# Second mixer's turned banks, work at the stage borders and the last norm put in another order: a float32 network of two blocks on one Trainium2 core

## Chip, core and metric

The kernel runs on one core of a Trainium2 chip. The metric is the device time of one execution in microseconds (us). Everything is float32. The weights come from HBM in each execution; activations stay in SBUF.

## What is computed

The input is 256 tokens of width 1024. A first block (a SwiGLU "ffn1", a mixer of RWKV-7 and dilated attention, a SwiGLU "ffn2") is followed by two layers of a second block, which the change is about. Cut to its core:

```python
def second_layer(x, i):                                   # i = 0, 1
    z = h @ w_in                                          # dq, dk, dv, cq, ckv, kr, gates
    o_a = rmsnorm((softmax(dq1 @ dk1.T) - lam * softmax(dq2 @ dk2.T)) @ dv)   # 8 heads
    o_b = softmax(q_mla @ k_mla.T) @ v_mla                # 8 heads, from low-rank cq, ckv
    m = g_a * (o_a @ w_branch_diff) + g_b * (o_b @ w_branch_mla)
    x = layernorm(ALPHA * x + m @ w_out)                  # "norm 2i"
    f = swiglu(x) if i == 0 else moe(x)                   # dense 2816, or 8 experts of 3584, top 2
    e = sigmoid(x @ w_ple_gate) * (p[i] @ w_ple_proj)     # p[i]: 256 x 256 embedding
    x = layernorm(ALPHA * x + f + e)                      # "norm 2i + 1"
```

## The kernel before

The 256 tokens are two tiles `t` of 128. `h_cm` holds the activations with channels on partitions (8 groups `k`), `x_tm` and `xn` with tokens on partitions. Every float32 product is two records per 128-row step in the trace, so a gate product of one token tile and 512 columns (8 groups) counts as 16 pieces. The program gives each engine its own list of instructions, in an order written out by hand, tied by semaphores; nothing reorders it at run time.

**Banks.** `next_bank()` deals the eight PSUM banks in turn. `fill` makes TensorE wait until the bank's last user has been copied out, `full` makes a reader wait for the product, `free` and `drained` tell and await the copy. ScalarE and VectorE share the copies.

**Weights.** One list, `stream`, names every slab of weights in the order of use; SyncE (SP) loads them into four slots in turn (line 2861), each load waiting for the last reader of the load four places ahead. Dense FFNs (`sp_ffn`) and the experts (`sp_experts`) load two pieces per unit of 256 hidden columns, of 2 MB and 1 MB.

**ffn2** (`dve_ffn`, `dve_unit`, line 608). 11 units; TensorE does the up products of unit u + 1, then the down product of unit u (`pe_up`, `pe_down`). VectorE multiplies gate and up when a unit's up products are ready, and then does `beside(u)`: an eleventh of the relative bias table (`dve_bias`, lines 1820 to 1828). After the last unit it adds the four result banks to `x_tm` (line 686); TensorE turns `x_tm` for the second block (line 394).

**Second mixer** (`pe_mixer2`, `act_mixer2`, `dve_mixer2`). For each pair of heads `a`: `dqk(a)` (query and key product), `diff_scores(a)` (line 1922), softmax on VectorE and ScalarE, and later `diff_out(a)`, which turns the weights into two banks (line 1931), waits until both are copied to `PT2` (ScalarE line 2090, VectorE line 2227) and multiplies them with the values (lines 1940, 1941). `mla_out(g)` does the same with three banks (lines 1966, 1976, 1978; copies in lines 2097 and 2252). Products of other weights (`dv`, `uq`, `ukv`, the gates `g2`) stand between. ScalarE takes its copies in its own fixed order: in `mla_out(1)` it copies the turned banks and the output, then takes the root of the mean squares (line 2147); VectorE inverts it (line 2276) and scales OA (line 2279), which `bdiff` reads. `pe_out` multiplies the merged branches with `w_out` (line 1637), and the embedding `ple` is turned (line 2047).

**Behind the mixer** (`pe_extras`, `dve_extras`). VectorE adds `w_out`'s products, takes the norm tile by tile (lines 2288, 1838 to 1844), TensorE turns `x_tm` (line 394), ScalarE and VectorE copy it to `h_cm`. Four gate products (`pg`) and four small projections (`pp`, all after them) follow, both through line 321; VectorE multiplies and adds them (lines 2350, 2352). In layer 0 the dense FFN follows in the seven-product form of line 443: it needs sums of the inputs and of each unit's weights, which VectorE makes (`dve_x_sums`, `dve_weight_sums`, lines 561 to 577) before TensorE's third product. In layer 1 a router goes between, and then 16 gather products and a transpose (line 2529, 2534), before which TensorE waits for all eight banks.

**Experts and tail.** 112 units (lines 2483, 2495), one pass. Last, the sums of expert 7 are turned (line 2509), copied by ScalarE (half 0) and VectorE (half 1) (line 2594), scattered by four products (line 2573) and, per token tile, added (line 2670), reduced to mean and variance (2671 to 2674), and normed in three operations of 1024 columns (2677, 2679, 2680). One DMA stores both tiles (line 2863).

## Time and profile before

| what | value |
|---|---|
| three runs | 2799.74, 2808.26 (median), 2810.09 us |
| the profiled execution | 2807.01 us; its span in the trace 2805.1 us |
| busy, share of the span | TensorE matmul 2696.7 us (96%), weight load 2272.9 (81%), VectorE 892.8 (32%), ScalarE 366.6 (13%), GpSimd 19.6 (1%) |
| mean granted TensorE clock | 0.993 |
| DMA | 601.6 MB, 214 GB/s over the span; in the slices of the experts 369 to 401 GB/s |

The span begins with the first instruction and ends with the last DMA. A row of a timeline or group gives the line of the kernel, engine, operation, out<-in by the program's names, sizes and a count of records; behind it, in brackets, the idle time of the engine before it and what ended that. PEclk is the share of the full TensorE clock that was granted. `SPq` is SyncE's DMA issue. The border between ffn2 and the second block lies at 943 us, layer 0 of the second mixer runs to 1239, layer 1 from 1499 to 1788, the experts from 1855 to 2782.

### The profile page before, as it was taken

Reading aid. Unit: us, or ns where it says so; the run is one execution under the profiler, and the core shown is the slowest. Engines: PE = TensorE matmul, PEld = TensorE weight load, DVE = VectorE, ACT = ScalarE, POOL = GpSimd, SP = SyncE. Lnnn points to the kernel's source line nnn. Section 1 sums busy time; section 2 is a strip of 40 time slices with the busy share of each in tenths; the row PEclk is TensorE's granted clock in tenths of the full one; section 3 lists DMA queues with packets and bytes.
Section 4 is the critical chain, followed back from the end, with each engine's and each line's share of the span. In section 5 each row is a group of like instructions: output and inputs, shape, how many; then the busy total and the mean of one; then the engine's idle time right before and its main releaser. Section 6 shows DMA issues by size and latency. Waiting matters only on the chain.

```text
span 2805.1 us, 73047 instructions
## 1 busy us (share of the span) xinstructions
PE 2696.7 (96%) x33424; PEld 2272.9 (81%) x33424; DVE 892.8 (32%) x1661; ACT 366.6 (13%) x827; POOL 19.6 (1%) x36
## 2 busy tenths in 40 slices
PE   7999999899999999999999999999999999999997
PEld 6877778877677768857876788479999999999997
DVE  5341554623776433425443334320000000000003
ACT  1002232210100034200002241110000000000000
POOL 0000000000000000000000000000000000000000
PEclk9999999999999999999999999999999999999999
DMA  5434332022443424333445243259999999999995
GB/s 196 180 150 181 118 121 84 4 80 109 148 177 138 176 100 152 120 135 121 179 159 197 98 154 121 90 225 397 369 379 396 387 396 374 370 401 376 397 386 237
DMA packets 55573, 601.57 MB, mean 214 GB/s; under 512 B 6320, under 2 KB 6448, under 8 KB 9856
## 3 DMA queue, kind: packets, MB, share of 16 engines
q1 hardware_dynamic: 52128, 587.74, 53.5%
q0 software_dynamic: 3296, 11.57, 1.2%
q8 instruction: 127, 2.08, 0.3%
q14 instruction: 22, 0.18, 0.0%
HBM read 595.48 MB, written 3.81 MB: 214 GB/s over the span
## 4 chain that ended last, share of the span: by engine, by line
PE 91%; DMA 4%; DVE 3%; issue 1%; ACT 1%; SPq 0%; DVEq 0%; ACTq 0%
PE bank L311 21%; PE bank L2483 19%; PE bank L443 10%; PE bank L2495 9%; PE bank L475 7%; PE bank L321 6%; PE bank L464 5%; DMA slot<-in_experts 4%; PE bank L1637 3%; PE bank L1203 2%; PE bank L1623 1%; PE bank L2529 1%; PE bank L931 1%; PE bank L1224 1%; PE bank L1296 0%
## 5 line engine op out<-in xcount | busy, mean ns | idle before, releaser
L2483 PE MATMUL bank<-arena,slot 128*64 128x96 f32 x14336 | 615.4, 246 | 10.1 <-issue 6.1
L2483 PEld LDWEIGHTS bank<-arena,slot 128*64 128x64 f32 x14336 | 601.4, 137 | 14.0 <-issue 13.9
L311 PE MATMUL bank<-h_cm,slot 128*128 128x256 f32 (+2 forms) x2032 | 447.5, 381 | 0.3 <-ACT h_cm L350 0.3
L311 PEld LDWEIGHTS bank<-h_cm,slot 128*128 128x128 f32 (+2 forms) x2032 | 383.9, 190 | 63.2 <-issue 8.2
L2495 PE MATMUL bank<-ff,slot 128*64 128x96 f32 x7168 | 320.8, 246 | 14.6 <-DMA slot<-in_experts 8.2
L2495 PEld LDWEIGHTS bank<-ff,slot 128*64 128x64 f32 x7168 | 306.5, 137 | 17.6 <-issue 17.6
L2643 DVE TENSOR_TENSOR ff<-ff,bank 128x192 f32<-128x192 f32 x112 | 39.6, 354 | 797.4 <-PE bank L2483 797.4
L475 PE MATMUL bank<-slot,ff 128*128 128x512 f32 x528 | 231.5, 592 | 0.0
L475 PEld LDWEIGHTS bank<-slot,ff 128*128 128x128 f32 x528 | 98.8, 190 | 112.4 <-issue 111.9
L464 PE MATMUL bank<-h_cm,slot 128*128 128x256 f32 x704 | 153.7, 379 | 0.4 <-ACT h_cm L352 0.4
L464 PEld LDWEIGHTS bank<-h_cm,slot 128*128 128x128 f32 x704 | 133.7, 190 | 22.5 <-issue 4.9
L1828 DVE SCALAR_TENSOR_TENSOR arena<-arena 128x384 f32<-128x384 f32 x264 | 142.7, 613 | 1.2
L321 PE MATMUL bank<-slot,h_cm 128*128 128x512 f32 (+1 forms) x320 | 136.4, 585 | 1.3 <-ACT h_cm L350 1.1
L2607 ACT ACTIVATE ff<-bank 128x192 f32<-128x192 f32 x112 | 37.1, 331 | 768.5 <-PE bank L2483 768.5
L311 PE MATMUL bank<-arena,slot 128*128 128x256 f32 x608 | 133.2, 380 | 0.0
L443 PE MATMUL bank<-arena 128*128 128x128 f32 x1056 | 126.9, 277 | 4.2 <-DVE arena L574 4.2
L311 PEld LDWEIGHTS bank<-arena,slot 128*128 128x128 f32 x608 | 115.0, 190 | 18.3 <-issue 2.9
L443 PEld LDWEIGHTS bank<-arena 128*128 128x128 f32 x1056 | 123.1, 194 | 4.5 <-DVE arena L574 4.5
L321 PEld LDWEIGHTS bank<-slot,h_cm 128*128 128x128 f32 x320 | 61.2, 194 | 71.2 <-issue 70.4
L443 PEld LDWEIGHTS bank<-h_cm,slot 128*128 128x128 f32 x704 | 81.8, 192 | 10.7 <-issue 10.7
L443 PE MATMUL bank<-h_cm,slot 128*128 128x128 f32 x704 | 82.2, 275 | 1.2 <-DVE h_cm L365 1.2
L1637 PE MATMUL bank<-slot,arena 128*128 128x512 f32 x192 | 82.9, 592 | 0.0
(402 smaller groups left out, 2025.4 us busy)
## 6 DMA issues: line engine op xcount, KB each, us to landing
slot<-in_experts SPq DMA_DIRECT2D x112, 2048.0 KB, 9.0
slot<-in_experts SPq DMA_DIRECT2D x112, 1024.0 KB, 9.2
slot<-in_ffn SPq DMA_DIRECT2D x22, 2048.0 KB, 9.2
slot<-in_ffn SPq DMA_DIRECT2D x22, 1024.0 KB, 4.9
slot<-in_dense SPq DMA_DIRECT2D x11, 2048.0 KB, 8.9
slot<-in_dqk SPq DMA_DIRECT2D x8, 2048.0 KB, 8.1
slot<-in_g SPq DMA_DIRECT2D x8, 2048.0 KB, 7.8
slot<-in_w_in_rkv SPq DMA_DIRECT2D x6, 2048.0 KB, 7.9
```

The lines of the kernel that those rows point to most:

```text
L311: ins = pe.matmul(ps[0:m, j * S:(j + 1) * S], w[:, k * width + c0:k * width + c0 + m], rhs[:, k, :], start=k == 0, stop=k == ks - 1)
L321: ins = pe.matmul(ps[:, 0:n], lhs[:, k, t * P:(t + 1) * P], w[:, k * width + c0:k * width + c0 + n], start=start and k == 0, stop=stop and ...
L443: ins = pe.matmul(ps[:, g, :], left[q][:, k, g, :], right[q][:, k, :], start=k == 0, stop=k == 3)
L464: ins = pe.matmul(bank[:, m * S:(m + 1) * S], slot[s][:, c0:c0 + P], h_cm[:, k, :], start=k == 0, stop=k == KD - 1)
L475: ins = pe.matmul(PS[4 + 2 * t + half][:, :], hidden[par][:, kk, t * P:(t + 1) * P], slot[s][:, kk * D + half * 512:kk * D + half * 512 + ...
L1203: ins = pe.matmul(ps[rows, h * width + c0:h * width + c0 + 64], left(rows, a, p, i), right(rows, a, p, i), start=True, stop=True)
L1637: ins = pe.matmul(ps[:, :], src[:, k, t * P:(t + 1) * P], w[:, k * 512:(k + 1) * 512], start=k == 0, stop=k == KD - 1)
L1828: v.scalar_tensor_tensor(BIAS[:, h, :], REACHED[r], STEP_NOW[:, r * 8 + h:r * 8 + h + 1], BIAS[:, h, :], ALU.mult, ALU.add).then_inc(done, 1)
L2483: ins = pe.matmul(bank[64 * c:64 * c + 64, m * PLACES:(m + 1) * PLACES], slot[s][:, c0:c0 + 64], QUEUE[:, e, k, :], start=k == 0, stop=k = ...
L2495: ins = pe.matmul(PS[down_bank(e) + d // 4][64 * c:64 * c + 64, (d % 4) * PLACES:(d % 4 + 1) * PLACES], slot[s][:, c0:c0 + 64], ff[:, 2 + ...
L2607: act.activation(ff[:, par, 0:2 * PLACES], PS[par][:, 0:2 * PLACES], ACT.Silu).then_inc(silu_ready, 1)
L2643: v.tensor_tensor(ff[:, 2 + par, 0:2 * PLACES], ff[:, par, 0:2 * PLACES], PS[2 + par][:, 0:2 * PLACES], ALU.mult).then_inc(hidden_ready, 1)
```

## The change

Seven edits. (1) In the second mixer the turning transposes become functions of their own (`diff_turn`, `mla_turn`), and the next scores, or half of the last gate product, are put between them and the product that uses the turned banks. (2) In ffn2 `beside(u)` comes before unit u's multiply; `beside(1)` also before unit 1's. (3) The embedding is turned before `w_out`, copied by VectorE in the mixer, and half of the projections go before the norm's transposes, the other half between the gate products; their slab is loaded first. (4) In layer 0 VectorE makes the dense FFN's input sums and first weight sums before it multiplies the gate products. (5) The gathers start in the bank that is next in turn and wait for each bank by itself; two banks are passed over in layer 1. (6) The scatter is ordered by half, and the last norm has two operations of 1024 columns instead of three. (7) Each token tile is stored by itself; ScalarE releases the first store.

```diff
@@ -246,12 +246,12 @@
                             ("bdiff_", 0), ("bdiff_", 1), ("out2_", 0), ("out2_", 1)):
                 stream.append(((f"{name}{l}", n), dram[f"{name}{l}"][n], dram[f"{name}{l}"].shape[2]))
             if l == 0:
+                slabs("pleproj_0")
                 slabs("plegate_0")
-                slabs("pleproj_0")
                 stream.append(("ffn", "dense", U_DENSE))
             else:
+                slabs("pleproj_1")
                 slabs("plegate_1")
-                slabs("pleproj_1")
                 stream.append(("experts", "experts", N_EXPERTS * U_EXPERT))
...
@@ -618,28 +618,33 @@
         def dve_ffn(dve, name, beside=lambda u: None):
 
             n0 = unit_base[name]
-            for j in range(2):
-                dve_unit(dve, (n0 + j) % 2, n0 + j, True)
-                beside(j)
+            dve_unit(dve, n0 % 2, n0, True)
+            beside(0)
+            beside(1)
+            dve_unit(dve, (n0 + 1) % 2, n0 + 1, True)
             with dve.Fori(1, U_DENSE // 2) as i:
                 for j in range(2):
+                    beside(i * 2 + j)
                     dve_unit(dve, (n0 + j) % 2, i * 2 + n0 + j, False)
-                    beside(i * 2 + j)
+            beside(U_DENSE - 1)
             dve_unit(dve, (n0 + U_DENSE - 1) % 2, n0 + U_DENSE - 1, False)
-            beside(U_DENSE - 1)
...
+        def dve_unit_sums(dve, name, j, i=0):
+            at = first_load[name] + 2 * j
+            dve_weight_sums(dve, U_DENSE * IN_SEVEN[name] + j + 2 * i, at // SLOTS + 1 + i, at % SLOTS)
+
+        def dve_first_sums(dve, name, turned):
+            h_written(dve, turned)
+            dve_x_sums(dve, IN_SEVEN[name])
+            dve_unit_sums(dve, name, 0)
...
@@ -1923,13 +1932,15 @@
                                             KDF[64 * m:64 * m + 64, 2 * a + j, 0:n], start=True, stop=True)
                         filled(ins, key)
 
-            def diff_out(a):
+            def diff_turn(a):
                 pe.wait_ge(named("diff_weights"), 4 * l + a + 1)
                 for b, blocks in enumerate((range(0, 4), range(4, 6))):
                     ps = fill(pe, ("dt", l, a, b), next_bank())
                     for i, f in enumerate(blocks):
                         ins = pe.transpose(ps[:, i * P:(i + 1) * P], WD[:, f // 3, (f % 3) * P:(f % 3 + 1) * P], ident)
                     filled(ins, ("dt", l, a, b))
+
+            def diff_out(a):
                 for b in range(2):
                     drained(pe, ("dt", l, a, b))
                 for t in range(T):
...
@@ -1991,12 +2004,14 @@
                     ins = pe.matmul(ps[:, j * S:(j + 1) * S], ones, LSQ[:, k, :], start=k == ks[0], stop=k == ks[-1])
             filled(ins, ("ls", l))
             dqk(1)
+            diff_turn(0)
+            diff_scores(1)
             diff_out(0)
-            diff_scores(1)
             dv(1)
             dqk(2)
+            diff_turn(1)
+            diff_scores(2)
             diff_out(1)
-            diff_scores(2)
             pe.wait_ge(named("lat_ready"), l + 1)
             w = slab(pe, (f"uq_{l}", 0))
             for b in range(2):
...
                 product_tm(pe, ("uv", l, t), next_bank(), w, 1024, 512, 512, LAT[:, NQ:, :], NKV, t)
             released((f"ukv_{l}", 0), ("uv", l, 1))
             g2(0)
+            diff_turn(3)
+            mla_scores(0)
             diff_out(3)
-            mla_scores(0)
             g2(1)
+            mla_turn(0)
+            mla_scores(1)
             mla_out(0)
-            mla_scores(1)
             g2(2)
             pe.wait_ge(named("oa_squared"), l + 1)
             for b in range(4):
                 ps = fill(pe, ("dn", l, b), next_bank())
                 filled(pe.matmul(ps[:, :], ones, QD[:, 2 * b:2 * b + 2, :], start=True, stop=True), ("dn", l, b))
+            mla_turn(1)
+            g2_bank(3, 0)
             mla_out(1)
-            g2(3)
+            g2_bank(3, 1)
             for g in range(2):
                 drained(pe, ("mo", l, g))
             w = slab(pe, (f"bmla_{l}", 0))
@@ -2039,13 +2059,13 @@
                     product_cm(pe, ("bd", l, 4 * s + 2 * j), next_bank(), w, 512,
                                [(2 * j * P, P), ((2 * j + 1) * P, P)], OA, KD)
                 released((f"bdiff_{l}", s), ("bd", l, 4 * s + 2))
-            pe_out(pe, f"out2_{l}", KDF, "merged", 4 * l)
             pe.wait_ge(named("ple_loaded"), 16 * (l + 1))
             ps = fill(pe, ("pleT", l), next_bank())
             for k in range(2):
                 for t in range(T):
                     ins = pe.transpose(ps[:, k * S + t * P:k * S + (t + 1) * P], PLE_TM[:, t, k * P:(k + 1) * P], ident)
             filled(ins, ("pleT", l))
+            pe_out(pe, f"out2_{l}", KDF, "merged", 4 * l)
 
         def act_softmax(act, l, name, groups, base):
...
@@ -2280,6 +2300,8 @@
             for tile in range(0, 16, 2):
                 drained(dve, ("g2", l, tile))
             dve_merge(dve, ch, ("bm", l), ("bd", l), gates2, KDF, QD, (8, 0))
+            ps = full(dve, ("pleT", l))
+            free(v.tensor_copy(PLE_CM, ps[:, :].rearrange("p (k s) -> p k s", s=S)), ("pleT", l))
 
         def dve_add_mix(dve, l, t, half):
             key = (f"out2_{l}", half, t)
...
@@ -2310,22 +2336,24 @@
                     ins = pe.matmul(ps[:, c0:c0 + 8], const(lhs, P), RT[4][:, t, :], start=start, stop=stop_)
                 filled(ins, ("rank",))
 
+            drained(pe, ("pleT", l))
+            projection(0)
+            pe_layernorm(pe, 2 * l)
             for s in range(2):
+                if s:
+                    projection(1)
+                    released((f"pleproj_{l}", 0), ("pp", l, 1, 1))
                 w = slab(pe, (f"plegate_{l}", s))
                 for t in range(T):
                     product_tm(pe, ("pg", l, s, t), next_bank(), w, 512, 0, 512, h_cm, KD, t,
                                turned=("turn", 2 * l + 1) if s == t == 0 else None)
                     if l == 1 and s == t == 0:
                         router()
+                        for held in range(2):
+                            next_bank()
                 released((f"plegate_{l}", s), ("pg", l, s, 1))
                 if l == 1 and s == 0:
                     ranks()
-            drained(pe, ("pleT", l))
-            w = slab(pe, (f"pleproj_{l}", 0))
-            for s in range(2):
-                for t in range(T):
-                    product_tm(pe, ("pp", l, s, t), next_bank(), w, 1024, 512 * s, 512, PLE_CM, 2, t)
-            released((f"pleproj_{l}", 0), ("pp", l, 1, 1))
 
         def act_extras(act, ch, l):
             for s in range(2):
@@ -2338,9 +2366,9 @@
 
         def dve_extras(dve, ch, l):
             v = nc.vector
-            ps = full(dve, ("pleT", l))
-            free(v.tensor_copy(PLE_CM, ps[:, :].rearrange("p (k s) -> p k s", s=S)), ("pleT", l))
-            if l == 1:
+            if l == 0:
+                dve_first_sums(dve, "dense", ("turn", 1))
+            else:
                 dve_router(dve, ch)
             for s in range(2):
                 for t in range(T):
...
             L, n0 = first_load["experts"], unit_base["experts"]
             gathered, scattered = named("moe_bank_filled"), named("moe_scattered")
-            for b in range(8):
-                pe.wait_ge(psum_free[b], turns[b])
+            moe_from.append(rotation[0] + 1)
             assert 2 * U_EXPERT % SLOTS == 0
             with pe.Fori(0, passes(pe)) as p:
 
                 pe.wait_ge(named("ln_var"), p * T + T * LAST_NORM)
                 pe.wait_ge(named("pick_ready"), p + 1)
                 for j in range(GATHERS + TURNED):
-                    ps = PS[j % 8]
-                    if j >= 8:
+                    ps = PS[moe_first(j)]
+                    if j < 8:
+                        pe.wait_ge(psum_free[moe_first(j)], turns[moe_first(j)])
+                    else:
                         pe.wait_ge(named(f"moe_bank_read{j % 2}"), p * moe_reads(j % 2) + (j - 8) // 2 + 1)
                     if j < GATHERS:
                         k, h = divmod(j, 2)
@@ -2566,10 +2600,10 @@
 
                 pe_moe_turn(pe, p, N_EXPERTS - 1)
                 pe.wait_ge(hidden_ready, p * ALL_UNITS + n0 + ALL_UNITS)
-                for half in range(2):
-                    pe.wait_ge(sums_ready[half], p * N_EXPERTS + N_EXPERTS)
                 for b in range(4):
-                    t, half = divmod(b, 2)
+                    half, t = divmod(b, 2)
+                    if t == 0:
+                        pe.wait_ge(sums_ready[half], p * N_EXPERTS + N_EXPERTS)
                     pe.matmul(PS[b][:, :], RETURN[:, t * P:(t + 1) * P], SUMS[:, LAST, half * 512:half * 512 + 512],
                               start=True, stop=True).then_inc(scattered, 1)
...
@@ -2619,6 +2653,9 @@
                 for t in range(T):
                     act.wait_ge(named("ln_var"), p * T + T * LAST_NORM + t + 1)
                     act.activation(lstd[:, t:t + 1], lstd[:, t:t + 1], ACT.Sqrt).then_inc(named("ln_std"), 1)
+                act.wait_ge(named("out_row0"), p + 1)
+                act.copy(stat[:, 13:14], ident[:, 0:1])
+            act.copy(stat[:, 14:15], ident[:, 0:1]).then_inc(named("first_ready"), 1)
 
         def dve_experts(dve, ch):
...
+                tail = named("tail_step")
+
+                def tail_done(n):
+                    dve.wait_ge(tail, p * TAIL_STEPS + n)
+
+                def tail_add(t, half):
+                    c = slice(half * 512, half * 512 + 512)
+                    dve.wait_ge(named("moe_scattered"), p * 4 + 2 * half + t + 1)
+                    v.tensor_tensor(E_TM[:, t, c], E_TM[:, t, c], PS[2 * half + t][:, :], ALU.add).then_inc(tail, 1)
+
+                def tail_stats(t, half):
+                    v.bn_stats(bnst[:, t, 6 * half:6 * half + 6], E_TM[:, t, half * 512:half * 512 + 512]).then_inc(tail, 1)
+
+                def tail_var(t, n):
+                    v.tensor_copy(lstd[:, t:t + 1], bnst[:, t, 0:1])
+                    v.bn_aggr(bnag[:, t, :], bnst[:, t, :]).then_inc(tail, 1)
+                    tail_done(n)
+                    v.tensor_scalar(lstd[:, t:t + 1], bnag[:, t, 1:2], EPS, None, ALU.add).then_inc(named("ln_var"), 1)
+
+                def tail_rows(t, n):
+                    dve.wait_ge(named("ln_std"), p * T + T * LAST_NORM + t + 1)
+                    v.reciprocal(lstd[:, t:t + 1], lstd[:, t:t + 1]).then_inc(tail, 1)
+                    v.scalar_tensor_tensor(OUT[:, t, :], E_TM[:, t, :], bnag[:, t, 0:1], lnrow[:, 0, :], ALU.subtract, ALU.mult
+                                           ).then_inc(tail, 1)
+                    tail_done(n + 2)
+                    v.scalar_tensor_tensor(OUT[:, t, :], OUT[:, t, :], lstd[:, t:t + 1], lnrow[:, 1, :], ALU.mult, ALU.add
+                                           ).then_inc(named(f"out_row{t}"), 1)
+
+                for half in range(2):
+                    for t in range(T):
+                        tail_add(t, half)
+                tail_done(3)
+                tail_stats(0, 0)
+                tail_stats(0, 1)
+                tail_done(6)
+                tail_var(0, 7)
+                tail_stats(1, 0)
+                tail_stats(1, 1)
+                tail_done(9)
+                tail_var(1, 10)
+                dve.wait_ge(named("ln_rows"), 16 * 2 * (LAST_NORM + 1))
+                tail_rows(0, 10)
+                tail_rows(1, 12)
                 for t in range(T):
...
+                    dve.wait_ge(named(f"out_row{t}"), p + 1)
             dve.sem_inc(named("out_ready"), 1)
 
...
+            sp.wait_ge(named("first_ready"), 1)
+            sp.dma_start(out[:, 0, :], OUT[:, 0, :]).then_inc(named("out_stored"), 16)
             sp.wait_ge(named("out_ready"), 1)
-            sp.dma_start(out, OUT).then_inc(named("out_stored"), 16)
-            sp.wait_ge(named("out_stored"), 16)
+            sp.dma_start(out[:, 1, :], OUT[:, 1, :]).then_inc(named("out_stored"), 16)
+            sp.wait_ge(named("out_stored"), 32)
```

`mla_out` is divided as `diff_out` is, `dve_ffn_seven` no longer makes the first sums, `g2` is divided into `g2_bank(s, j)`, and the two halves of `projection(s)` are `product_tm` of the two token tiles.

## Rows read from the trace of the kernel before

**Rows 1.** Waits of TensorE, whole span: engine, line <- releaser: total us, times, longest us.
```profile
PE bank L2495 <- DMA slot<-in_experts: 8.2, 7, 2.1
...
PE bank L1940 <- ACT arena L2090: 5.0, 8, 0.8
...
PE bank L394 <- DVE x_tm L686: 3.4, 1, 3.4
...
PE bank L1976 <- DVE arena L2252: 3.3, 4, 0.8
```

**Rows 2.** Stretches: us, busy us of PE, PEld, DVE, ACT, POOL, clock, DMA share, GB/s.
```profile
1861.00:2777.00 916.00, 891.95 (x21306) 884.55 (x21304) 52.90 (x129) 44.21 (x125) 7.44 (x11) 1.00 0.96 385
...
1240.00:1241.00 1.00, 1.00 (x2) 0.34 (x1) 1.00 (x2) 0.98 (x2) 0.00 (x0) 0.50 0.88 377
```

**Rows 3.** Timeline of VectorE and TensorE, start of ffn2: start us, us, engine, line.
```profile
735.73 0.69 DVE L608 TENSOR_TENSOR ff<-ff,bank 128x512 f32<-128x512 f32 x1 [0.90 <-ACT ff L548]
...
750.80 0.69 DVE L608 TENSOR_TENSOR ff<-ff,bank 128x512 f32<-128x512 f32 x1
...
763.92 7.03 PE L475 MATMUL bank<-slot,ff 128*128 128x512 f32 x16
```

**Rows 4.** Chain of waits behind ffn2: start us, us, what.
```profile
946.67 3.75 PE bank L394 x16
...
950.42 35.78 PE bank L311 x160
```

**Rows 5.** Timeline of ScalarE and VectorE between MLA output and OA, layer 0.
```profile
1151.52 0.59 ACT L2099 COPY arena<-bank 128x512 f32<-128x512 f32 x1 [1.76 <-PE bank L1978]
...
1155.36 12.95 DVE L2276 RECIPROCAL arena<-arena 128x2048 f32<-128x2048 f32 x1 [5.90 <-ACT arena L2147]
...
1170.68 1.29 DVE L2279 TENSOR_SCALAR arena<-arena,cols 128x2048 f32<-128x2048 f32 x1
```

**Rows 6.** Timeline of TensorE, from embedding transposes to dense FFN, layer 0.
```profile
1234.24 0.60 PE L2047 MATMUL bank<-consts,arena 128*128 128x128 f32 x4
...
1237.63 1.09 PE L394 MATMUL bank<-consts,x_tm 128*128 128x128 f32 x8 [1.91 <-DVE x_tm L1844]
...
1239.27 29.19 PE L321 MATMUL bank<-slot,h_cm 128*128 128x512 f32 x64 [0.55 <-ACT h_cm L350]
...
1268.29 7.03 PE L321 MATMUL bank<-slot,arena 128*128 128x512 f32 x16
...
1281.95 5.47 PE L443 MATMUL bank<-arena 128*128 128x128 f32 x32 [3.06 <-DVE arena L574]
```

**Rows 7.** Timeline of VectorE, first input sum and last weight sum, dense FFN.
```profile
1276.88 0.69 DVE L561 TENSOR_TENSOR arena<-h_cm 128x512 f32<-128x512 f32 x1
...
1282.94 1.22 DVE L577 TENSOR_TENSOR arena<-slot,arena 128x1024 f32<-128x1024 f32 x1
```

**Rows 8.** Timeline of TensorE, gathers of the experts.
```profile
1831.94 22.60 PE L2529 MATMUL bank<-arena,x_tm 128*128 128x384 f32 x64 [2.50 <-issue]
```

**Rows 9.** Timeline of the tail; third, 1024-wide scalar_tensor_tensor of line 2439 (ns).
```profile
2784.13 0.69 DVE L2594 COPY arena<-bank 96x512 f32<-96x512 f32 x1 [1.09 <-PE bank L2509]
...
2786.10 0.69 DVE L2670 TENSOR_TENSOR arena<-arena,bank 128x512 f32<-128x512 f32 x1 [1.28 <-PE bank L2573]
...
L2439 DVE SCALAR_TENSOR_TENSOR arena<-arena x4: 1277/1281/1285, 2761.7 to 2765.5; 128x1024 f32<-128x1024 f32 x4
...
2797.21 0.81 DVE L2677 TENSOR_SCALAR arena<-arena,ff 128x1024 f32<-128x1024 f32 x1
...
2799.32 1.23 DVE L2680 TENSOR_TENSOR arena<-arena,xn 128x1024 f32<-128x1024 f32 x1
...
2800.79 0.35 SPq L2863 DMA_DIRECT2D out<-arena  x1
```

**Rows 10.** DMA issues of the page: size of one, median us to landing.
```profile
slot<-in_bdiff SPq DMA_DIRECT2D x4, 2048.0 KB, 7.8
...
slot<-in_pleproj SPq DMA_DIRECT2D x2, 1024.0 KB, 4.9
```

63 lines of the change are left out of this document (26 added, 37 removed).

## Prediction

> **What bounds the kernel now.** I read the waits of TensorE first, because its matmuls fill nearly the whole span: what it waits for is what can be won. The reader is to see that the waits are short and lie at borders: eight waits for a turned attention bank (5.0 us), four for the second kind (3.3), one for the bias work of VectorE (3.4) [rows 1]. Next come the stretches: the loop over experts takes 916 of 2805 us, and there TensorE (892) and the DMA engines (0.96) are both full; one microsecond of a border elsewhere shows TensorE at a granted clock of 0.50, the 1.2 GHz level, where nearly everything else has 1.00 [rows 2]. So the loop of experts is left as it is, and the change is worth what it takes from the borders, plus the slow clock behind them. The timelines of the borders give the terms. All sums are made against the profiled execution (2807.01 us, span 2805.1), which stands 1.25 us under the median of the three runs (2808.26).
>
> **Term A, the ffn2 stage.** Each `beside` is 750.80 - 735.73 - 0.6 = 14.5 us of VectorE [rows 3]. Two of them now precede unit 1's product: it ends at 736.4 + 2 x 14.5 + 0.7 = 766.0. TensorE wants it (`down` of unit 1) at 763.9, so a new wait of about 2.0 us appears; behind VectorE nothing else is queued, and ScalarE's next silu waits only for unit 0. A unit costs TensorE 20.7 us (up 64 x 0.215, down 16 x 0.43) and VectorE 15.2, so VectorE has caught up two units later, and the wait comes once. At the other end VectorE no longer has 14.5 us of bias after the last unit. `down` ends at 946.67 - 3.4 = 943.3 [rows 1, 4]; the first three additions then lie under `down` itself, the fourth takes 0.7 under the first eight transposes. A piece of 512 columns takes 0.43 us (16 in 7.03, with a drain of some 0.15 [rows 3]), one of 256 a half, one of 128 a quarter, 0.11. So sixteen transposes take 1.8 us against 3.4 + 3.75, and the product of 160 pieces 34.5 against 35.78. From 943.3 to the end of that product: 42.9 before, 36.4 after: 6.5 gained, 2.0 paid. **4.5**.
>
> **Term B, the two mixers.** In each layer, four `diff` and two `mla` turns now have scores (or, last, half a gate product) between the transposes and their use, at least 16 pieces of 0.1 us, while the copy of a bank takes 0.59 [rows 5]. The 5.0 and 3.3 us go [rows 1]. What is late next: the scores wait for ScalarE's copy of the `dqk` bank, done just as six transposes end; I take zero. Banks: laid out over the eight, each is reused at least one product after its copy. **8.3**, between 4 and 8.3. The last move delays something: the MLA output bank comes half a gate product (6.9 us) later, and ScalarE stands waiting for it, with the square root queued behind it, for which VectorE's reciprocal of 12.95 us waits. Before, the output bank ends at 1151.5 and OA is ready at 1172.0, 20.5 us later [rows 5]. After, TensorE goes on from the output with 6.9 (half gate) + 13.8 (`bmla`) = 20.7 us and then wants OA. A slack of 27.6 - 20.5 = 7.1 us shrinks to 0.2: cover still, but only just.
>
> **Term C, layer 0 behind the mixer.** Before [rows 6]: the products with `out2` end at 1234.4 (the embedding's transposes begin), gate product starts at 1239.27 (4.85 us later), 64 pieces in 29.0 instead of 27.5 (slow clock, 1.5), projections 6.9 to 1275.3; then 32 pieces of the FFN, a wait of 3.06 for the weight sums, and 32 pieces in 5.47, to 1287.25: 52.8 us. After: turning the embedding, now ahead of the products out, 0.45; half of the projections 3.43 and the first eight transposes 0.86 fill the norm's wait (z of the second tile is there after 3.2); second transposes to product 1.64 (1239.27 - 1237.63); gates 27.5; other projections 3.43; FFN's banks 0 to 3 free 1.4 later (0.6 of ScalarE, 0.7 of VectorE on the last piece; bank 2 is one of them); 64 pieces of 0.11, 7.15. Sum 45.9. **6.9**. The input and first weight sums move under the gate product: x sums and four weight sums run 1276.88 to 1284.16, 7.3 us [rows 7]. Before the first multiply they end at about the 19th microsecond, the second projection wants its bank at 20: no wait, under 1 us if the slab lands late. SP's queue: the projection's slab comes first, the second gate slab is asked for 6.9 us before the products out end and needed 20 us after; the first dense slab is behind it, asked for as before. POOL issues nothing new.
>
> **Term D, layer 1.** The same border gives 4.85 + 1.6 + 3.43 - 6.4 = 3.5. At the gathers, before: idle 2.5, then 64 pieces of 384 columns in 22.6, of which 20.6 at full clock [rows 8]. The wait for all banks (0.8) goes; I keep the 1.7 between bank and first gather, which nothing in the trace explains. 25.1 against 22.3: 2.8. **6.3**. The loads of experts start on the end of the first `up`, as before: the loop shifts as a whole.
>
> **Term E, the tail.** The first addition starts at 2786.10; the scatter now begins with ScalarE's half alone, which is turned four transposes (0.5) before the half that VectorE copies until 2784.8; so 0.5 sooner, bounds 0 and 0.7. From it to the last row was 14.45. After: additions paced by the scatter 3.3, four statistics 2.9, two variances 0.9, reciprocals 0.4, four `scalar_tensor_tensor` of 1024 at 1.28 with hops 5.2: 12.7. So 0.5 + 1.75. ScalarE's reply (0.2) is hidden under tile 1. Per tile 0.81 + 1.23 + 1.22 = 3.26 becomes 2.56 [rows 9]. The store ends 4.3 us after its issue; half the bytes save between 0 and 2.15: loads of 2 MB and 1 MB land in 7.8 and 4.9, so half a MB is worth 1.4, which I take [rows 10]. **3.7**. VectorE's two operations each read two tensors. The Trainium skill (VectorE: DVE Perf Modes, the perf-mode tier table) has fp32 `tensor_scalar` at two elements per cycle and `tensor_tensor` at one, so the change gives up the only fast pass; by its figures, halved for 1024, an estimate is 0.61 + 2 x 1.15 = 2.91 against 2.3, 0.6 saved per tile and not 0.7. The rows have the same two rates. For the store, the skill (DMA: Bandwidth & Descriptors, Anatomy of one DMA) states about 2.0 us fixed plus bytes at 436 GB/s; by that the half store would save 1.2.
>
> **Sum.** 4.5 + 8.3 + 6.9 + 6.3 + 3.7 = 29.7; 2807.0 - 29.7 = 2777.3, and as a median 1.25 more: 2778. The clock: I count no fall behind the waits that remain (2.0, 1.7, 1.4, 0.6), since the one of 2.1 us in the expert loop stood at 1.00 [rows 1, 2], while 3.4, 3.06, 2.5 and 1.91 with 0.55 were followed by a fall. Each fall costs 1.5 to 2.0.
>
> **Rivals.** (1) *The waits move.* The clock falls as often as before (four times 1.6), and half of B comes back as waits for `dqk` copies and banks. For it: the mixer's copies follow each other on one engine. Against: the eight-bank order. 29.7 - 6.4 - 4.2 = 19: 2789. (2) *OA comes late.* The slack of 0.2 is overdrawn by a table load of 1.28 and hops in both layers, and the FFN wait of 2.0 brings a fall: 3 + 1.6: 2782. (3) *Slower: the expert loop loses its balance with the DMA.* 112 units of 3.15 MB took 8.18 us each at 385 GB/s [rows 2]. Its loads begin in another slot order than before. If the DMA engines gave 366 GB/s, a unit would take 8.59, and 112 of them 46 us more: 2824. It decides from 0.27 us per unit, where all the gain is gone. Against: the order of loads after the first unit is unchanged, and TensorE itself needs 7.96 of the 8.18. (4) *It does not overlap.* The projection or the sums ahead are held by a bank or slab, so C and D give a third: 2787.
>
> **How the numbers follow.** Forecast 0.64, (1) 0.15, (2) 0.08, (4) 0.08, (3) 0.03, the last 0.02 among waits I do not see. A measurement of this kernel tells about 0.5% from no change, 14 us: 2794. Forecast, (2), nearly all of (4) and most of (1) lie under it: faster 0.91, same 0.06, slower 0.03. Range: up to rival (1) and the half of the runs' spread (10 us); down, 2778 - 5 for the spread and - 7 for the 1.7 at the gathers, the FFN bank wait, the store's bound and a better loop: 2766 to 2793.
>
> **What would show it.** Right: no waits of the lines that use turned banks; one new wait of about 2 us on the second `down` of ffn2; the gate products 6.4 us behind the products out with clock 1.00; no wait on the weight sums in the first dense unit; a first store under the work of tile 1. Wrong: a wait of `bdiff` on OA; clock 0.50 behind the borders; the loop from first expert product to last longer than 921 us.

## The result, and the profile after

The changed kernel takes 2775.97 us (median of 4 runs, 2770.60 to 2781.55) against 2807.60 in the runs beside it (2799.74 to 2810.09): a ratio of 0.9892, 95% interval 0.9864 to 0.992, so 1.1% faster, beyond the noise. Forecast were 2778 and 2766 to 2793. The profiled execution took 2774.82 us, span 2773.0, 32.1 under that of before.

TensorE's longest waits, and that of the second FFN, after the change (engine, line <- releaser: total us, times, longest):

```profile
PE bank L394 <- DVE xn L382: 16.6, 3, 12.9
PE bank L2511 <- issue: 8.3, 12, 1.3
PE bank L2523 <- DMA slot<-in_experts: 7.5, 6, 1.9
...
PE bank L475 <- DVE ff L608: 1.8, 1, 1.8
```

The waits for turned banks [rows 1] are gone, and that for the bias work at the FFN's end. One has come: `down` of unit 1, for VectorE's multiply. The timelines of the places where the prediction has a term, first the start and the end of ffn2 and of the first product behind it (start us, us, engine, line, shapes, xcount, idle before):

```profile
764.83 7.13 PE L475 MATMUL bank<-slot,ff 128*128 128x512 f32 x16 [1.76 <-DVE ff L608]
...
944.10 0.38 PE L394 MATMUL bank<-consts,x_tm 128*128 128x128 f32 x2
945.05 1.75 PE L394 MATMUL bank<-consts,x_tm 128*128 128x128 f32 x14 [0.57 <-DVE x_tm L691]
946.97 35.11 PE L311 MATMUL bank<-h_cm,slot 128*128 128x256 f32 x160 [0.17 <-ACT h_cm L354]
...
1139.49 1.47 PE L1977 MATMUL bank<-consts,arena 128*128 128x128 f32 x12
1140.81 7.07 PE L311 MATMUL bank<-h_cm,slot 128*128 128x256 f32 x32
1147.81 0.65 PE L1989 MATMUL bank<-arena 128*64 128x256 f32 x4
```

Against [rows 3, 4]: a wait of 1.76 where 2.0 was forecast; 3.75 us of slow transposes are 2.1 fast ones; but only two of them run before the wait of 0.57, not eight. The last three rows are the last turn of layer 0 (L1977), half a gate product, and the product over the turned banks, which starts without a wait. Next VectorE and ScalarE behind the MLA output of layer 0 [rows 5]:

```profile
1149.38 0.58 ACT L2119 COPY arena<-bank 128x512 f32<-128x512 f32 x1 [7.79 <-PE bank L1991]
...
1153.21 12.95 DVE L2296 RECIPROCAL arena<-arena 128x2048 f32<-128x2048 f32 x1 [11.92 <-ACT arena L2167]
...
1168.53 1.29 DVE L2299 TENSOR_SCALAR arena<-arena,cols 128x2048 f32<-128x2048 f32 x1
```

OA is ready at 1169.82. The product over it follows 20.73 us of other products (96 pieces) that follow one another from 1149.33, so it is wanted at 1170.06: 0.24 us of slack, where 0.2 was worked out. Then TensorE at the border of layer 0 [rows 6]:

```profile
1229.05 1.91 PE L394 MATMUL bank<-consts,x_tm 128*128 128x128 f32 x16
1231.51 13.97 PE L321 MATMUL bank<-slot,h_cm 128*128 128x512 f32 x32 [0.55 <-ACT h_cm L350]
1245.31 3.60 PE L321 MATMUL bank<-slot,arena 128*128 128x512 f32 x8
1248.75 13.90 PE L321 MATMUL bank<-slot,h_cm 128*128 128x512 f32 x32
1264.21 3.81 PE L443 MATMUL bank<-h_cm,slot 128*128 128x128 f32 x32 [1.57 <-issue]
```

The idle time of the norm is filled, the gate products run at full clock, and of the 3.06 us on the sums only 1.57 on bank 2 are left. Last the border of layer 1 and the gathers [rows 8], and three stretches of it (us, busy of PE, PEld, DVE, ACT, POOL, granted clock, DMA share, GB/s):

```profile
1769.49 7.10 PE L321 MATMUL bank<-slot,h_cm 128*128 128x512 f32 x16 [0.55 <-ACT h_cm L350]
1776.44 3.63 PE L2326 MATMUL bank<-arena,h_cm 128*128 128x8 f32 x32
1779.93 8.81 PE L321 MATMUL bank<-slot,h_cm 128*128 128x512 f32 x16
...
1806.86 20.80 PE L2563 MATMUL bank<-arena,x_tm 128*128 128x384 f32 x64
```

```profile
1774.00:1780.00 6.00, 6.00 (x40) 4.57 (x38) 0.98 (x1) 1.88 (x2) 1.06 (x2) 1.00 0.55 171
1780.00:1784.00 4.00, 4.00 (x7) 1.70 (x7) 3.00 (x18) 1.12 (x2) 0.00 (x0) 0.57 0.01 5
1784.00:1790.00 6.00, 6.00 (x23) 3.25 (x22) 1.12 (x8) 0.96 (x2) 0.00 (x0) 1.00 0.15 30
```

The gathers start without a wait and at full clock. But behind the router's 32 narrow matmuls (8 columns) the clock goes to the 1.2 GHz level, though TensorE was never idle: the same gate product takes 7.10 us ahead of them and 8.81 behind.

Where the 32.1 us went, each from the starts of products in both timelines: 1.0 ahead of everything that was changed; **A** 3.1; **B** 9.9; **C** 6.75; **D** 6.5; the expert loop, 926.97 before and 926.12 after, 0.85; **E** 4.4; less 0.4 in the first products of layer 1, which the clock fall around norm 1 meets at another point.

### The profile page after: what moved, and what is told of

Same layout as the page of the kernel before. It is cut to its first block, busy times and chain, and to the rows that moved or that the text cites. A ratio compares the mean times of both kernels' runs of the same rounds, so it can differ in the third digit from the quotient of the medians.

```text
span 2773.0 us, 73042 instructions
## 1 busy us (share of the span) xinstructions
PE 2689.7 (97%) x33424; PEld 2268.6 (82%) x33424; DVE 890.5 (32%) x1659; ACT 365.2 (13%) x829; POOL 19.6 (1%) x36
## 4 chain that ended last, share of the span: by engine, by line
PE 91%; DMA 4%; DVE 3%; issue 1%; ACT 1%; POOL 0%; SPq 0%; DVEq 0%; POOLq 0%; ACTq 0%
PE bank L311 21%; PE bank L2511 19%; PE bank L443 10%; PE bank L2523 9%; PE bank L475 8%; PE bank L321 6%; PE bank L464 4%; DMA slot<-in_experts 4%; PE bank L1642 3%; PE bank L1208 2%; PE bank L1628 1%; DVE arena L1833 1%; PE bank L2563 1%; PE bank L936 1%; PE bank L1229 1%
```

## The experiments

Stretches repeat from profile to profile to some 0.02 us where neither a wait nor the granted clock differs, while whole executions scatter by 10. So each experiment is read at its own stretch. These are TensorE's, in us, start to start: `down` of unit 0 to the transposes behind ffn2; those to the first product of layer 0; out product to the first dense `down`; the mixer of layer 0; gate product to the gathers; gathers to the first expert; and from the end of the last product to the end of the span.

```
kernel               ffn2  turn   border 0  mixer 0  gates 1  gathers  end
before             203.43  3.55     98.34   220.65    43.37    23.55  16.47
after              201.88  2.87     91.16   216.12    37.37    21.75  12.64
e1_late_out        202.15  2.87     91.15   225.96    35.66    21.76  12.59
e2_bias_later      199.85  2.87     91.15   216.13    37.36    21.76  12.62
e3_sums_back       201.82  2.87     93.22   216.13    39.02    21.76  12.61
e4_all_banks       202.13  2.87     91.18   216.13    40.61    23.52  12.69
e5_mixer_alone     203.42  3.55     96.86   215.69    43.37    21.86  16.39
e6_banks           201.38  2.27     89.34   216.13    37.36    21.76  12.65
e7_router_spread   200.73  2.87     91.15   216.13    35.66    21.76  12.64
e8_one_store       200.73  2.87     91.15   216.13    39.02    21.76  13.93
e9_best            199.85  2.28     89.35   216.13    35.67    21.76  12.62
e10_router_thrice  201.84  2.87     95.41   216.13    49.39    21.75  12.60
e11_after_again    206.40  2.87     91.15   216.13    39.02    21.76  12.67
e12_banks_bias     199.86  2.28     89.35   216.13    37.37    21.75  12.68
```

**e1: is OA just in time?** One line moved:

```
             g2_bank(3, 0)
-            mla_out(1)
             g2_bank(3, 1)
+            mla_out(1)
```

> The changed kernel with one product less under the chain behind the second MLA group: both halves of the last gate product stand ahead of its output, where the change has the output between them. Theory (the OA chain is just in time): its output, the square root, the reciprocal of 12.95 us and the two multiplies all come 6.9 us later, while the branch products that stand ahead of the first user of OA start at most 1.1 us later (the wait for the output's copy). OA was ready 0.24 us before it was wanted, so the product over OA waits 5.5 to 6.7 us in each of the two layers, named as a wait for DVE, and the mixers together cost 13 to 14 us more than in the changed kernel; a clock fall behind each wait may add about 1.5 us each. Rival (the chain is hidden with more room than the trace suggests): no wait of the product over OA above 1 us, and the total within 2 us of the changed kernel.

Measured: 2798.45 us; the timeline at the product over OA, and the clock behind its start:

```profile
1162.10 14.05 PE L311 MATMUL bank<-arena,slot 128*128 128x256 f32 x64 [0.73 <-issue]
1181.91 30.92 PE L311 MATMUL bank<-arena,slot 128*128 128x256 f32 x128 [5.76 <-DVE arena L2299]
```

```profile
1182.00:1184.00 2.00, 2.00 (x5) 1.64 (x6) 2.00 (x4) 0.00 (x0) 0.00 (x0) 0.50 0.31 131
...
1186.00:1188.00 2.00, 2.00 (x6) 1.60 (x5) 0.00 (x0) 0.00 (x0) 0.00 (x0) 0.50 0.00 0
1188.00:1190.00 2.00, 2.00 (x10) 1.73 (x9) 0.00 (x0) 0.00 (x0) 0.00 (x0) 0.98 0.00 0
```

The wait is within the theory's 5.5 to 6.7, and it is 5.76 in layer 1 too. The fall behind it is dearer than I said: 9.84 us in layer 0, less 5.76 and 0.73, leave 3.3; in layer 1 it was 8.97 us in all, which leaves 2.5. With the output 6.9 us later the mixer of layer 0 takes 225.96, over 5 us more than before the change (220.65). The change sits 0.24 us from that edge.

**e2: is the new wait in ffn2 one bias piece too early?**

```
             beside(0)
-            beside(1)
             dve_unit(dve, (n0 + 1) % 2, n0 + 1, True)
+            beside(1)
```

> The changed kernel with the bias pieces of the second FFN shifted by one unit: multiply 0, bias 0, multiply 1, bias 1, bias 2, multiply 2, then one bias ahead of each multiply as in the change. Theory (the 1.8 us wait of the second down product comes from two bias pieces lying ahead of the multiply of unit 1, and one piece later there is room): unit 1 is multiplied near 751 us instead of 764, unit 2 near 780.5 against the 784.6 at which its down product starts, so the wait of 1.76 us of the down product on DVE's ff is gone and the FFN ends 1.7 to 1.9 us sooner (last down product ends near 942.3 against 944.12), with the gain at the end of the FFN kept. Rival (the time lost early is made up by the loop's loads or by the pace of DVE, so the FFN's end is set elsewhere): the wait goes but the last down product still ends within 0.4 us of 944.12, or another wait of 1 us or more stands at unit 2.

Measured: 2777.82 us as a whole, but the stage 199.85 against 201.88. Two rows in the place of the waiting one:

```profile
749.36 13.98 PE L464 MATMUL bank<-h_cm,slot 128*128 128x256 f32 x64
763.17 7.03 PE L475 MATMUL bank<-slot,ff 128*128 128x512 f32 x16
```

The wait is gone and none stands at unit 2; the rival fails, and e9 and e12 have the same 199.85. In the kernels that keep the change's order this wait took 0.6 (e7, e8) to 3.23 us (e11), so the edit is worth 0.9 to 6.5 us, by the execution; in e11 the clock fell behind it and `down` took 10.18 us:

```profile
764.62 10.18 PE L475 MATMUL bank<-slot,ff 128*128 128x512 f32 x16 [3.23 <-DVE ff L608]
```

The traces show why it varies. VectorE starts its bias work only when the load of `lambdas` has landed, and with it comes everything up to unit 1's multiply:

```profile
717.86 0.29 DVE L1775 CAST arena<-arena 128x256 f32<-128x256 int32 x1 [4.12 <-DMA arena<-in_lambdas]
```

That is 5.02 us behind TensorE's first up product in e11 and 3.55 in the first profile of the change, 1.47 later, and the wait is 1.47 longer. In e7 and e8 the clock fell ahead of ffn2, TensorE reached the first `down` 1.0 to 1.2 us later, and the wait is 1.15 shorter.

**e3: what are the early sums worth?** In `dve_extras` of layer 0, `dve_first_sums` behind the loop over the gate products again.

> The changed kernel with one part of layer 0's border undone: DVE makes the sums of x and of the first weights of the dense FFN behind the sums of the gate products again, as before the change. Theory (of the 6.9 us of that border 3.06 are the wait for the sums, and the clock fell behind it): the wait of about 3 us ahead of the dense FFN's products is back (less the 1.57 us that the changed kernel waits there for a bank), and behind it the clock falls to 0.50 for 2 to 3 us, which costs another 1.2 to 1.7: the first dense down product starts 2.7 to 3.5 us later than 1289.46. Rival (idle of this length alone does not bring the clock down, as the idles of 1.8 and 1.57 us in the changed kernel did not): granted clock stays at 1.00 and only 1.5 to 2.0 us are lost. A second rival (the sums were covered already, and the border's gain came from the projection in the norm's shadow alone): less than 0.5 us.

Measured: 2781.95 us; the stretch 2.06 longer.

```profile
1267.62 3.81 PE L443 MATMUL bank<-h_cm,slot 128*128 128x128 f32 x32 [1.57 <-issue]
1273.24 3.84 PE L443 MATMUL bank<-arena 128*128 128x128 f32 x32 [1.81 <-DVE arena L574]
```

```profile
1272.00:1274.00 2.00, 0.76 (x6) 0.76 (x7) 2.00 (x2) 0.00 (x0) 0.00 (x0) 1.00 0.00 0
1274.00:1276.00 2.00, 2.00 (x20) 2.00 (x19) 1.97 (x4) 0.00 (x0) 0.00 (x0) 1.00 0.00 0
```

My theory fails and the first rival holds (its upper end was 2.0): the wait on the bank hides part of that on the sums, and the clock stays.

**e4: what were the 1.7 us ahead of the gathers?** Nothing but this, ahead of reading the number of passes:

```
             moe_from.append(rotation[0] + 1)
+            for b in range(8):
+                pe.wait_ge(psum_free[b], turns[b])
```

> The changed kernel with the old wait ahead of the expert loop put back: TensorE's queue waits for all eight PSUM banks before it reads the number of passes and enters the loop; nothing else is changed. The last reader of a bank is the multiply of the last gate product, which starts 0.8 us behind the product's end and takes 0.69. Theory Q (the 1.7 us of the idle of 2.5 us before the change that no wait explains is the read of the register and the entry of the loop, which the wait for the banks kept from running under the products): the gathers start 2.3 to 3.3 us behind the last product's end, the idle put down to issue, and the experts start that much later. Rival B (only the wait for the banks costs, and the rest was something else of that place): the gathers start 1.3 to 1.6 us behind the product's end. Rival 0: below 0.5 us.

Measured: 2775.16 us as a whole, and

```profile
1807.66 22.57 PE L2565 MATMUL bank<-arena,x_tm 128*128 128x384 f32 x64 [3.08 <-issue]
```

Theory Q: 3.08 us idle. The multiply that reads the last bank ends at 1805.93, 1.4 us behind the product (1804.58); the other 1.7 is what stands between the old waits and the first gather in TensorE's list, the read of the register and the entry of the loop, which those waits kept from running ahead. The run doesn't divide the two. A fall costs 1.77 more (22.57 against 20.80). So this line alone is worth 5.0 us (40.61 + 23.52 - 37.37 - 21.75), yet the whole came out no slower: from the first expert to TensorE's last product, where the kernels do the same, it took 929.5 us here and 931.7 in the first profile of the change, and the part ahead of ffn2's first `down` was 2.6 shorter.

**e5: the mixers alone.** The kernel before, with only the split and the new order of `diff_turn`/`diff_out` and `mla_turn`/`mla_out`.

> The kernel before with one part of the change alone: in both mixers the transposes of a head group's weights stand ahead of the next scores (or of half a gate product), its output behind them. Theory (each part acts by itself, and the mixers' gain is the eight waits of 0.5 to 0.8 us on the transposed banks plus short gaps at the following products): from the end of the first product of each mixer to the start of its out product 4.7 to 5.1 us less in each layer (220.74 before; 216.23 in the changed kernel, which has 0.45 us of other work in it), some 9.9 us together, and every border between stages as before the change within 0.3 us. The prediction's own figure for this part was 8.3. Rival (part of the mixers' gain comes from the other edits, such as the banks' rotation or the moved loads): below 8.3 us together.

Measured: 2800.32 us. 4.96 us less in layer 0 and 4.95 in layer 1, 9.9 in all. But not every border is within 0.3 us of before. Border 0 is 1.48 shorter with the same instructions; that is the clock fall of [rows 2], which this execution lacks there. In layer 1 it lacks it too, and the one behind the idle time ahead of the gathers (21.86 against 23.55); there the clock falls behind the router instead, so that the gate stretch is 43.37 again:

```profile
1779.29 7.11 PE L321 MATMUL bank<-slot,h_cm 128*128 128x512 f32 x16 [0.55 <-ACT h_cm L350]
1786.23 3.63 PE L2315 MATMUL bank<-arena,h_cm 128*128 128x8 f32 x32
1789.72 8.81 PE L321 MATMUL bank<-slot,h_cm 128*128 128x512 f32 x16
...
1822.66 20.90 PE L2544 MATMUL bank<-arena,x_tm 128*128 128x384 f32 x64 [2.41 <-issue]
```

So the fall behind the router is not of the change's making, and the same borders of the same kernel meet a fall in one execution and none in another.

**e6: the banks.** `rotation[0] = 7` at the head of `pe_mixer2`.

> The changed kernel with the rotation of PSUM banks set back to its first bank at the start of both mixers, so that the first transposes of each go to banks 0 to 3 and not to those that hold the FFN's last results (4 to 7), and the last projection of layer 0 goes to banks 3 and 4 and not to bank 2, which the dense FFN's first products want. Theory (three short waits are bank conflicts and nothing else): the wait of 0.57 us in the first turn goes and half of the turn runs under the last sums, 0.6 to 0.9 us sooner at the first product (946.97); the wait of 1.57 us ahead of the dense FFN goes, and its first down product starts 1.3 to 1.6 us sooner by the stage's own clock; the turn behind the dense FFN starts up to 0.9 us sooner. Together 2.4 to 3.4 us. Rival (DVE's sums are what is late, and the banks only name it): the waits are named differently but the stages' starts move by less than 0.4 us each.

Measured: 2776.80 us; 0.60 at the turn behind ffn2 and 1.82 at the dense FFN's opening (the theory had up to 1.6), nothing behind the dense FFN:

```profile
948.36 2.10 PE L394 MATMUL bank<-consts,x_tm 128*128 128x128 f32 x16
...
1266.14 3.73 PE L443 MATMUL bank<-h_cm,slot 128*128 128x128 f32 x32
...
1479.25 1.05 PE L394 MATMUL bank<-consts,x_tm 128*128 128x128 f32 x8
1483.56 1.09 PE L394 MATMUL bank<-consts,x_tm 128*128 128x128 f32 x8 [3.26 <-DVE x_tm L1849]
```

Together 2.4 us. At the first two places the bank was the cause. At the third the rival holds: waits of 0.16, 0.87 and 1.78 became one of 3.26 on VectorE's norm.

**e7: the clock behind the router.** Each pair of narrow matmuls laid behind a pair of wide ones of the first two gate products; the ranks behind the projection.

```
+                for k in range(KD):
+                    ins = pe.matmul(ps[:, 0:512], h_cm[:, k, r * P:(r + 1) * P], w[:, k * 512:k * 512 + 512],
+                                    start=k == 0, stop=k == KD - 1)
+                    last = pe.matmul(rt[:, r * 8:(r + 1) * 8], h_cm[:, k, r * P:(r + 1) * P], ROUTER[:, k * 8:(k + 1) * 8],
+                                     start=k == 0, stop=k == KD - 1)
```

> The changed kernel with the router's 32 narrow matmuls (128x8) laid one pair behind each pair of the 32 wide matmuls of the first two gate products of layer 1, not all in a row between them; the rank products move behind the second half of the projection. Theory N (the clock falls behind a stretch of 3.6 us of narrow matmuls alone, though TensorE is busy): with the wide ones in between, the granted clock stays at 1.00 from the norm's end to the gathers, the stretch from the start of the gate product (1769.49) to the first gather (1806.86, 37.37 us) shrinks by 1.6 to 1.9 us, and nothing waits for the later ranks, which have some 13 us of room. Rival L (the fall comes from the transposes and idle moments of the norm before it, some microseconds late, whatever runs next): the clock falls all the same between 1776 and 1785 and the stretch is within 0.4 us of 37.37. Rival R (the later router makes the ranks or the gathers wait): a wait of 1 us or more at the rank products or the gathers.

Measured: 2774.92 us; 35.66 us, as theory N says, with clock 1.00 over the border, and no wait at the ranks:

```profile
1768.00:1778.00 10.00, 9.45 (x42) 5.68 (x41) 6.39 (x6) 3.21 (x5) 1.06 (x2) 1.00 0.36 137
1778.00:1788.00 10.00, 10.00 (x38) 5.62 (x37) 0.43 (x3) 1.88 (x2) 0.00 (x0) 1.00 0.24 79
```

But e1, with the router in a row, also had 35.66. So one profile doesn't settle it.

**e8: the store.** Both rows in one store of 1 MB behind the second.

> The changed kernel with its two stores of the output joined into one of 1 MB behind the last row's norm, as before the change. Theory (the tail's part of the store is the smaller transfer at the end): from the issue of the last store to the span's end 4.2 to 4.4 us against 3.02, and from the last down product to the end 19.4 to 19.7 against 18.27, so 1.2 to 1.4 us more. Rival (the two halves collide, or the end is set by the write's fixed time alone): within 0.3 us of 18.27.

Measured: 2780.53 us; 13.93 against 12.64, 1.29 us. The prediction had 1.4. The Trainium skill (DMA: Bandwidth & Descriptors, Anatomy of one DMA) fits a transfer as a fixed time plus bytes at 436 GB/s; by that half a MB is an estimate of 1.2. The section has that fit for transfers that GpSimd issues, and these two are SyncE's; the trace's 1.29 is near it.

**e10: the router three times, and the projection uncovered.** `for again in range(3):` around the router's loops; for layer 0, `projection(0)` from ahead of the norm to just ahead of `projection(1)`. The extra router matmuls repeat the result.

> The changed kernel with two edits in places that don't meet. Layer 1: the router's 32 narrow matmuls are made three times over in the same bank (the same result). Work for work that costs 7.0 us (3.49 us a pass, start to start, at full clock). Theory N (a row of narrow matmuls brings the clock down although TensorE is busy): the granted clock falls to 0.50 inside this row already and stays down until the wide ones have run for some microseconds, so that the stretch from the gate product's start to the first gather grows by more than 10 us over the 35.7 without a fall, to 47 or more. Theory M (the falls come from the norm before it, late): the fall is as long as in the other runs, the stretch 44 to 46. Layer 0: the first half of the projection stands behind the norm, with the second, and not ahead of it. Theory: the norm's idle time is bare again, so that from the end of the out product to the start of the gate product TensorE has the 4.59 us of before and not 2.46 behind 3.44 of product; from out product start to the first dense down product 2.1 us more than 91.16, and 3.6 to 3.9 with a clock fall behind the idle time. Rival: what the move hides comes back elsewhere, below 1 us.

Measured: 2798.79 us. The router and its clock:

```profile
1786.86 15.76 PE L2327 MATMUL bank<-arena,h_cm 128*128 128x8 f32 x96
```

```profile
1790.00:1792.00 2.00, 2.00 (x20) 2.00 (x20) 0.00 (x0) 0.00 (x0) 0.00 (x0) 1.00 0.23 92
1792.00:1796.00 4.00, 4.00 (x21) 4.00 (x20) 0.00 (x0) 0.00 (x0) 0.00 (x0) 0.51 0.02 4
```

TensorE is busy throughout, and the clock falls inside the row, 5.2 us behind its start, and stays down until wide products have run for 3.2 us. The stretch of 49.39 us is over the 47 of theory N. In layer 0 the border is 4.25 us longer, a little over the 3.9 of the theory: 2.6 up to the start of the gate product, 1.7 behind it, where the clock was 0.65 from 1237 to 1240.

**e9, e11, e12: a better version, beside the change.** e9 has the edits of e2, e6 and e7; e12 those of e2 and e6; e11 is the changed kernel unaltered.

> The changed kernel with three edits at once: the bias pieces one unit later (1.76 us in its own run), the rotation of banks set back at both mixers (0.60 and 1.81), and the router's matmuls spread between the wide ones of the gate product. Together 4.2 us from the first two at places that don't meet, and from the third what the clock fall behind the router costs: 1.7 us on its usual look, 3.35 on some, 0 on one. Theory N (narrow matmuls in a row bring the clock down): the stretch from the gate product's start to the first gather is 35.7 us again, as in the one run with the router spread, and the whole is 5.5 to 7.5 us faster than the changed kernel. Theory M (that run missed the fall by luck, as one of seven with the router in a row did): the stretch is 37.4 or 39.0, and the whole is 4 to 4.5 us faster. Rival (the expert loop, which waits for its loads, gives the time back): less than 2 us.

> The changed kernel with the bias pieces one unit later and the banks' rotation set back, the router's matmuls left in a row: 1.76 + 0.60 + 1.81 = 4.2 us less than the changed kernel. The router's stretch shows a clock fall (37.4 or 39.0 us from the start of the gate product to the first gather) under theory N in most looks. Against the kernel that has the router spread as well: 1.3 to 3.3 us slower under N, the same within 0.5 under theory M (the fall is luck).

> The changed kernel once more, for comparison on the same chip. The same stretches as in its first profile: 216.1 us from the fold of the rotary key to the out product in each mixer, 2.87 from the last down product to the first product of layer 0, 12.6 from the last product to the end; the router's stretch 37.4 or 39.0 us (a clock fall), 35.7 if it is missed. The whole within 0.2% of its 2775.97.

Measured, five runs each, against the same runs of before: e9 2772.73 us, ratio 0.9871 (0.9849 to 0.9893); e12 2776.67, 0.9891 (0.9873 to 0.9909); e11 2779.20, 0.9896 (0.9877 to 0.9915). The intervals overlap, so the whole times don't prove e9 the better; its stretches do for three of its parts: 2.03 in ffn2 (against the first profile of the change), 0.59 at the turn and 1.81 at border 0, 4.4 us in each of e9 and e12. For the fourth, e12 shows the fall (37.37), e11 too (39.02), e9 doesn't (35.67). With the router in a row and made once there are eleven profiles. Nine show a fall that begins 2.7 to 4.5 us behind the row's start: eight of the nine of the changed kernel's row, and e5. Two don't: e1, and the kernel before, where a fall had ended ahead of the row. Spread out, neither of two falls. If spreading did nothing, two misses would have a chance of about 1 in 30. That a row of narrow matmuls holds the clock down with TensorE busy is shown (e10: theory M had the fall no longer than elsewhere). That the row alone brings it down is likely but not shown, since all these rows follow the same norm; and that spreading keeps the clock up rests on two profiles, and would be worth 1.7 or 3.35 us.

## Why the prediction was right, and where its steps missed

The forecast, 2778, stands 2 us from the median (its own sum, 2777.3 and 1.25, is 2778.6), and no rival came true. The mechanism of every term is in the traces. That the total is so near is in part luck: A came out 1.4 low and B 1.6 high, and D is right by two misses. Term by term:

- **A**, 4.5 forecast, 3.1 measured. The wait at unit 1 was 1.76 for 2.0, and the stage lost 2.03 by it (e2). The end of the stage was mis-sized: 37.8 us from the last `down` to the end of the 160 pieces, for 36.4. "The fourth takes 0.7 under the first eight transposes" failed: one of the turn's four banks was the very one that held the fourth result; freed in e6, 0.60 came back. The rest is 0.6 us in the product (I priced it by a piece's rate alone) and the copy of the last turned bank, 0.17.
- **B**, 8.3 forecast, 9.9 measured, and 9.9 in e5. The step that was short is the price of a wait: the term took the listed lengths and no more. At the last turn of layer 0 the product behind it now starts 0.15 us before the modelled end of the transposes (1140.81 against 1140.96), as pieces do that follow one another unhindered; before, that overlap was lost with each wait. Over the six turns of a layer 4.95 us came back, for 4.17 of waits. "I take zero" for the `dqk` copies is right: 0.07 us at each of three scores. The slack of OA came out at 0.24 for 0.2, and e1 shows rival (2) is real: one half product more, and the mixer is slower than before the change.
- **C**, 6.9 forecast, 6.75 measured. Filling the norm's wait was worth 4.25, of which 1.7 are the clock behind it (e10), the early sums 2.06 (e3). The wait on bank 2, foreseen at 1.4, is 1.57.
- **D**, 6.3 forecast, 6.5 measured, by two misses that cancel. I kept 1.7 us ahead of the gathers as unexplained; e4 shows they hung on the wait for all banks, and they went. And I counted no clock fall where TensorE isn't idle; it fell behind the router and cost 1.7. The 1.6 that the term took for the norm's fall is no fixed gain either: e5 has the old order there and no such fall.
- **E**, 3.7 forecast, 4.4 measured: 0.55 at the first addition (0.5), 1.3 at the store (1.4, e8), and 2.6 in the norm against 1.75. The step that failed is the small work between the additions and the norm: 2.9 + 0.9 + 0.4 forecast, 3.5 measured, with the statistics in pairs of 1.28 and the rest closer behind. The two operations per tile took 2.58 for 2.56:

```profile
2757.82 0.69 DVE L2705 TENSOR_TENSOR arena<-arena,bank 128x512 f32<-128x512 f32 x1 [0.74 <-PE bank L2607]
...
2761.00 1.28 DVE L2708 BATCH_NORM_STATS2 ff<-arena 128x6 f32<-128x512 f32 x2
...
2765.79 1.28 DVE L2722 SCALAR_TENSOR_TENSOR arena<-arena,ff,xn 128x1024 f32<-128x1024 f32 x1
...
2767.49 0.34 SPq L2925 DMA_DIRECT2D out<-arena  x1
...
2769.98 0.34 SPq L2927 DMA_DIRECT2D out<-arena  x1
```

- The **expert loop** kept its balance: 926.12 us against 926.97, so rival (3) did not occur. My mark for it, "longer than 921 us", was set wrong, since the kernel before is over it, whether the last `down` is taken from its end (926.97) or its start (921.5).
- **Clock.** "I count no fall behind the waits that remain" held in the first profile (0.57, 1.57, 1.76), for the 1.81 of e3 and for 2.01 and 2.03 in ffn2 (e4, e1). It isn't safe for ffn2: that wait depends on when the load of `lambdas` lands, and at 3.23 us in e11 the stage lost 4.5 us more. Nor is the list of waits that were "followed by a fall" a rule: behind 2.41, and behind 1.91 with 0.55, e5 has none.
- **Signs.** The waits on turned banks are gone, one new wait stands at the second `down`, none on the weight sums, and the first store lies under tile 1's work, as said. The gate product starts 5.9 us behind the product out and not 6.4, since that figure counted the 0.45 of the embedding's turn, which by then lies ahead. One sign of being wrong came too: clock 0.50 behind a border, the one of layer 1.

The sum was right to 2.4 us (29.7 forecast, 32.1 measured, of which 1.45 net lie in stretches that were not changed).

## What to carry to other kernels

Put the transposes of a step ahead of independent products, and count how much cover is left behind every chain you delay: here one half product decided between 4.5 us won and 5.3 lost. When the rotation of banks meets stages with fixed banks, write out which bank each late result and each first product has; two of the three short waits left here were such a meeting. Judge edits of a few microseconds by the stretch they touch, from product start to product start, since stretches without a new wait or clock fall repeat to 0.02 us while parts untouched by any edit, such as the expert loop (929.5 to 937.4 us to the last product), move the whole by more.

## What the runs showed of the hardware that was not expected

- The granted clock of TensorE fell to the 1.2 GHz level with the engine busy throughout, behind or inside a row of matmuls of 8 columns: 32 of them cost 1.7 us, or 3.35 where the fall began inside the row (e3, e8, e11), and of 96 the later ones ran at 0.50 themselves (15.76 us). Laid between matmuls of 512 columns the same 32 cost nothing beyond their own time in two profiles.
- Narrow matmuls aren't the only such work. In the first block, which no edit touches, the clock also fell without any wait in five of the 14 profiles (e1, e3, e5, e6, e10), under products of 256 columns of which every other has 32 partitions; the stretch from 24.62 us became 29.38. In e3:

```profile
367.00:372.00 5.00, 5.00 (x10) 2.30 (x10) 4.34 (x2) 5.00 (x3) 0.00 (x0) 0.53 0.00 0
```

- Single waits of TensorE, over all 14 profiles from 700 to 2750 us (those with no other wait over 0.5 us within 12 us): behind none of the 236 of 0.5 to 1.91 us did the clock fall; behind six of the 18 from 1.92 to 2.50; behind all ten from 3.06 to 5.76. The fall cost 1.8 us behind 3.08 (e4), 3.1 behind 3.23 (e11), 3.3 and 2.5 behind 5.76 (the two layers of e1).
- Short waits close together are another matter: around the norm behind the dense FFN (0.87, 1.78 and mostly 0.55 us) the clock went to 0.50 in all eleven profiles that have them, and ahead of ffn2 (0.56 and 1.42) in five of 14.
- Taking a wait away gave back more than its length: 0.60 for 0.57, 1.82 for 1.57 (both e6), 2.03 for 1.76 (e2), and 0.83 a turn for waits of 0.70 on average (e5).
- The same instructions meet a fall in one execution and not in the next: from gate product to gathers, 35.66, 37.37 and 39.02 us are all found with the router in a row.
- The read of a register and the entry of a loop, together, cost TensorE some 1.7 us when a semaphore wait stands ahead of them in its queue (e4), and nothing visible when they can run under earlier matmuls.
